# Identity products around each normalization, and a gate projection whose first two blocks are cut at tile 13

## What is computed

```python
for i in range(DEPTH):
    mod = (silu(c) @ ada_w[i] + ada_b[i])
    sh1, sc1, g1, sh2, sc2, g2 = jnp.split(mod, 6, axis=-1)
    h = rms_norm(x, norm1_g[i]) * (1.0 + sc1) + sh1
    mix = dilated_attention(...) if i == 0 else s5_mixer(...)
    x = x + g1 * mix
    h = rms_norm(x, norm2_g[i]) * (1.0 + sc2) + sh2
    x = x + g2 * conv_ffn(h, ...)
return rms_norm(x, final_norm_g)

def s5_mixer(h, ...):
    u = h @ w_in
    y = scan_and_project(u) + d_skip * u      # 128 groups of 16 channels, 64 states each
    g = gelu(y)
    g = g * sigmoid(g @ w_gate)
    return g @ w_out
```

## Time and profile before

| | |
|---|---|
| median of 3 runs | 2860.27 us (2857.16 to 2860.38) |
| the profiled execution | 2856.33 us, its span 2854.5 us |
| TensorE | 2761.2 us busy (97%), mean granted clock 0.985 |
| VectorE | 2249.6 us busy (79%) |
| ScalarE | 1267.3 us busy (44%) |
| GpSimd | 466.5 us busy (16%) |

### The profile page before, as it was taken

The page is one execution under the profiler, slowest core; times in us unless marked ns, Lnnn a source line. Parts: engine busy times, 40 slices in busy tenths (PEclk is TensorE's granted clock), DMA queues, the critical chain, the costliest instruction groups (busy, mean ns, idle before and its releaser), DMA issues.

```text
span 2854.5 us, 52641 instructions
## 1 busy us (share of the span) xinstructions
PE 2761.2 (97%) x19980; PEld 2521.2 (88%) x19980; DVE 2249.6 (79%) x3003; ACT 1267.3 (44%) x1775; POOL 466.5 (16%) x461
## 2 busy tenths in 40 slices
PE   8799999999989999999999999989999999999998
PEld 3788888888889999999999998989878888888887
DVE  7887877777869988889888778987888875666655
ACT  1334444444434544434444334444355553455542
POOL 4061111011023111000111111234401110000121
PEclk9899999999999999999999999999999999999999
DMA  9989887787756888878888876768867766655563
GB/s 361 352 275 371 294 277 267 261 267 259 263 178 232 295 296 287 281 234 302 300 295 304 270 245 215 241 205 281 310 218 242 265 183 187 194 185 186 183 183 111
DMA packets 241693, 724.50 MB, mean 254 GB/s; under 512 B 50912, under 2 KB 59872, under 8 KB 240736
## 3 DMA queue, kind: packets, MB, share of 16 engines
q1 hardware_dynamic: 185184, 666.98, 68.9%
q10 hardware_dynamic: 56320, 54.93, 6.2%
HBM read 700.58 MB, written 25.43 MB: 254 GB/s over the span
## 4 chain that ended last, share of the span: by engine, by line
PE 87%; DVE 6%; issue 3%; DMA 2%; ACT 1%; POOL 1%; ACTq 0%; SPq 0%; DVEq 0%; POOLq 0%
PE proj L1827 31%; PE proj L1830 15%; PE proj L1832 11%; PE proj L1834 11%; PE proj L1833 11%; DVE acc L1025 2%; PE pmisc L1856 1%; PE proj L1826 1%; DMA raw<-in_w_in 1%; DMA ada<-in_ada_w 1%; DVE w_lo L1116 1%; PE ps L1915 1%; PE ps L1942 1%; PE proj L1915 1%; PE ps L2026 1%
## 5 line engine op out<-in xcount | busy, mean ns | idle before, releaser
L566 ACT ACTIVATE w_hi<-raw 128x1024 fp32r<-128x1024 f32 (+1 forms) x896 | 935.6, 1045 | 1411.3 <-PE proj L1834 580.0
L1116 DVE TENSOR_TENSOR w_lo<-raw,w_hi 128x1024 fp32r<-128x1024 f32 (+1 forms) x896 | 1107.1, 1236 | 467.1 <-ACT w_hi L566 462.3
L1827 PE MATMUL proj<-h_hl,w_hi 128*128 128x512 f32 x3232 | 1139.5, 400 | 6.5 <-DVE work L1294 3.9
L1830 PE MATMUL proj<-h_hl,w_lo 128*128 128x256 f32 x3030 | 851.5, 281 | 0.0
L1827 PEld LDWEIGHTS proj<-h_hl,w_hi 128*128 128x128 f32 x3232 | 599.0, 189 | 138.0 <-DVE work L1294 4.2
L1830 PEld LDWEIGHTS proj<-h_hl,w_lo 128*128 128x128 f32 x3030 | 574.6, 190 | 7.3
L1832 PE MATMUL proj<-h_hl,w_hi 128*128 128x256 f32 x1888 | 548.6, 291 | 30.0 <-DVE h_hl L1071 11.0
L1833 PE MATMUL proj<-h_hl,w_hi 128*128 128x256 f32 x1888 | 538.8, 285 | 0.0
L1834 PE MATMUL proj<-h_hl,w_lo 128*128 128x256 f32 x1888 | 538.6, 285 | 0.0
L1832 PEld LDWEIGHTS proj<-h_hl,w_hi 128*128 128x128 f32 x1888 | 366.1, 194 | 38.7 <-issue 12.7
L1025 DVE SCALAR_TENSOR_TENSOR acc<-ada,cs,acc 128x1024 f32<-128x1024 f32 x285 | 392.0, 1375 | 0.6 <-DMA ada<-in_ada_w 0.3
(11 more groups left out here) (259 smaller groups left out, 2441.9 us busy)
## 6 DMA issues: line engine op xcount, KB each, us to landing
raw<-in_w_up SPq DMA_DIRECT2D x352, 512.0 KB, 5.5
ada<-in_ada_w SPq DMA_DIRECT2D x348, 512.0 KB, 5.9
raw<-in_w_in SPq DMA_DIRECT2D x224, 512.0 KB, 5.8
raw<-in_w_down SPq DMA_DIRECT2D x128, 448.0 KB, 3.8
raw<-in_w_down SPq DMA_DIRECT2D x64, 512.0 KB, 3.8
raw<-in_w_out SPq DMA_DIRECT2D x32, 512.0 KB, 5.1
raw<-in_ssm_w_in SPq DMA_DIRECT2D x32, 512.0 KB, 4.9
raw<-in_ssm_w_gate SPq DMA_DIRECT2D x32, 512.0 KB, 5.7
```

The lines of the kernel that those rows point to most:

```text
L566: nc.scalar.activation(w_hi[:, j % LAG, 0:nk * P], raw[:, j % s.ring, 0:nk * P], ACT.Copy).then_inc(hi_ready, 1)
L1116: V.tensor_tensor(w_lo[:, j % LAG, 0:nk * P], raw[:, j % s.ring, 0:nk * P], w_hi[:, j % LAG, 0:nk * P].bitcast(F32), ALU.subtract).then_in ...
L1827: ins = mm(both, w_hi[:, j % LAG, w], hl[:, k].rearrange("p c t -> p (c t)"), start=(k == 0), stop=end)
L1830: ins = mm(o, w_lo[:, j % LAG, w], hi[:, k, :], start=False, stop=False)
```

## The change

Two edits. First, `stay_awake(count)` on TensorE issues float32 products of the identity with itself into `ps0`, whose result nobody reads: 8 ahead of `mean`, 10 between `mean` and `spread_root`, 4 behind, in normalizations 1 to 4. Second, in the gate stream TensorE takes piece 0, piece 2, then tiles 8 to 12 of piece 1 and tiles 8 to 12 of piece 3, and only behind these `outputs(14)` and `outputs(15)`, then tiles 13 to 15 of both pieces; `kernels_of(15)` comes ahead of these tiles. DVE gets `skip(13)` to `skip(15)` behind the `low` of step 3, and ACT gets all carried work of due 3 and later behind the `high` of step 3.

```diff
+LAST_TILES = {"heads": 2, "outputs": 3}
@@ ScalarE, gate stream
-            carry = run_steps(act, ..., carry=sooner(carry, 2), keep=True)
+            carry = run_steps(act, ..., carry=sooner(carry, 3), keep=True)
@@ VectorE, state-space stream and gate stream
-                late.setdefault(2 * n + 12, []).append(skip(n))
-            carry = run_steps(dve, ..., done=LO_FIRST, keep=True)
+                late.setdefault(2 * n + 12 if n < KT - 3 else 3 * KT + n, []).append(skip(n))
+            over = run_steps(dve, ..., done=LO_FIRST, keep=True)
+            carry = sooner({due: over[due] for due in over if due < KT}, 2)
+            carry[3] = [f for due in sorted(over) if due >= KT for f in over[due]]
-            carry = run_steps(dve, ..., carry=sooner(carry, 2), keep=True)
+            carry = run_steps(dve, ..., carry=carry, keep=True)
@@ TensorE, products
-                    if cross == "heads" and isinstance(i, int) and i == 0 and j in (1, 2, 3):
+                    if cross in LAST_TILES and isinstance(i, int) and i == 0 and j in (1, 2, 3):
                         if j == 1:
                             piece(i, 2, 0)
                         for n in (1, 3) if j > 1 else ():
-                            piece(i, n, 0 if j == 2 else 2 if n == 1 else 1, HEADS - 2, j == 3)
+                            piece(i, n, 0 if j == 2 else 2 if n == 1 else 1, KT - LAST_TILES[cross], j == 3)
@@ TensorE, norm
+            def stay_awake(count):
+                for _ in range(count):
+                    mm(ps0[:, 0:P], ident[:], ident[:], start=True, stop=True)
             def norm(number):
+                stay_awake(8)
                 mean(number)
+                stay_awake(10)
                 spread_root(number)
+                stay_awake(4)
@@ TensorE, state-space stream and gate stream
-                late.setdefault(2 * n + 7, []).append(outputs(n))
-            carry = run_steps(pe, ..., late, keep=True)
-            stream("gate", ..., True, sooner(carry, 1))
+                late.setdefault(2 * n + 7 if n < KT - 2 else 3 * KT + n, []).append(outputs(n))
+            over = run_steps(pe, ..., late, keep=True)
+            carry = sooner({due: over[due] for due in over if due < KT}, 1)
+            carry[2] = [f for due in sorted(over) if due >= KT for f in over[due]]
+            stream("gate", ..., "outputs", carry)
```

More of the change, by code:

```diff
@@ L978, in _ @@
                 late.setdefault(2 * b + 7, []).append(gate_high(b))
-            carry = run_steps(act, s.count, s.length, high(s), late, carry=sooner(carry, 2), keep=True)
+            carry = run_steps(act, s.count, s.length, high(s), late, carry=sooner(carry, 3), keep=True)
             load_taps(1)
@@ L1577, in _ @@
                 late.setdefault(2 * n + 9, []).append(turn_out(n))
-                late.setdefault(2 * n + 12, []).append(skip(n))
-            carry = run_steps(dve, s.count, s.length, low(s), late, done=LO_FIRST, keep=True)
+                late.setdefault(2 * n + 12 if n < KT - 3 else 3 * KT + n, []).append(skip(n))
+            over = run_steps(dve, s.count, s.length, low(s), late, done=LO_FIRST, keep=True)
+            carry = sooner({due: over[due] for due in over if due < KT}, 2)
+            carry[3] = [f for due in sorted(over) if due >= KT for f in over[due]]
             s = st["gate"]
@@ L1594, in _ @@
             take_parts(s, late)
-            carry = run_steps(dve, s.count, s.length, low(s), late, carry=sooner(carry, 2), keep=True)
+            carry = run_steps(dve, s.count, s.length, low(s), late, carry=carry, keep=True)
             split_first("up1a", residual("ssm_out", 1, 2 * KT, carry, keep=True))
@@ L2064, in _ @@
                 late.setdefault(2 * n + 5, []).append(kernels_of(n))
-                late.setdefault(2 * n + 7, []).append(outputs(n))
-            carry = run_steps(pe, s.count, s.length, products(s, h_hi, h_lo, h_ready(2), True), late, keep=True)
-            stream("gate", a_hi, a_lo, lambda k: pe.wait_ge(g_lo, k), True, sooner(carry, 1))
+                late.setdefault(2 * n + 7 if n < KT - 2 else 3 * KT + n, []).append(outputs(n))
+            over = run_steps(pe, s.count, s.length, products(s, h_hi, h_lo, h_ready(2), True), late, keep=True)
+            carry = sooner({due: over[due] for due in over if due < KT}, 1)
+            carry[2] = [f for due in sorted(over) if due >= KT for f in over[due]]
+            stream("gate", a_hi, a_lo, lambda k: pe.wait_ge(g_lo, k), "outputs", carry)
             stream("ssm_out", h_hi, h_lo, lambda k: pe.wait_ge(gg_lo, k))
```

## The result

| | before | after |
|---|---|---|
| median of 8 runs each | 2857.16 us (2854.91 to 2860.38) | 2866.62 us (2863.89 to 2869.96) |
| profiled execution, span | 2856.33, 2854.5 us | 2866.88, 2865.1 us |

The ratio is 1.0028, with the interval 1.0020 to 1.0037: the change makes the kernel 8.0 us slower (5.7 to 10.6). The forecast was +4.1 us.

A forecast was written before the change was run, and what follows sets the result against it. TensorE, busy 97% of the span, was taken to bound the kernel; +3.8 us for the gate part and +0.3 for the normalizations gave +4.1 on a 2860.3 us median, so 2864.4 us, range 2858.0 to 2869.0.

The forecast's parts named there:

- (D): Gate stage and normalizations: full clock returns late at 1887.5 and falls again among the tiles; +7.3 us, 2867.6; chance 0.17.
- D's +1.9: Normalizations: upper bound if the clock falls again while tiles are made, so the first three lose their last-tile gain.
- Steps 1 to 4: Gate stage: piece 1's tiles start at 1878.6; piece 3 waits for `low` until 1887.5, with outputs(14) and outputs(15) queued behind.
- Step 5: Gate stage: after the wait, five tiles at half clock take 3.3 us, both outputs at full clock 4.3; +3.8 us.
- my high end: Gate stage: the clock stays at half through outputs(14), which then costs its old 3.77 us; +5.4 us.
- the middle value: Gate stage: piece 3's five tiles at half clock, both outputs at full clock; outputs(15) ends at 1895.1, +3.8 us.
- by as much: Gate stage: whatever moves the end of outputs(15) moves the kernel's end equally, piece 4 trailing it by 9.6 us.
- Step 6: Gate stage: ACT's new order costs nothing; widen_c(15), ready about 1890.3, is covered by piece 3 and outputs(14), otherwise it binds.
- The normalizations: Normalizations 1 to 4: identity products at 0.22 us delay the spread, faster spread and last tiles give back; sum +0.3 us.
- (A): Gate stage: nothing waits for w_lo, ten tiles fill the idle stretches, outputs(15) starts 0.8 us earlier; 2859.8; chance 0.10.
- (B): Normalizations: identity products are cheap and hold the clock, -3.6 us, with the gate's +3.8; 2860.5; chance 0.12.
- (C): Normalizations: the ten products run at half clock, spread 3.4 us late, +13.5 over four; 2877.6 with the gate; chance 0.06.

The follow-up runs named there:

- gate: The changed kernel without any identity product, so the new gate order alone; against the kernel before 1.0020, +5.7 us.
- loads: The kernel before with the conditioning sum's tiles in the gate stream starting at step 6 instead of 4; 0.9982, -5.1 us.
- gate_p3: The new gate order alone, with only piece 1's tiles 8 to 12 ahead and all of piece 3 behind outputs(15); against the kernel before 1.0014, +4.0 us.
- gate_loads: The new gate order alone, with the conditioning sum's tiles starting at step 6 instead of 4; against the kernel before 0.9996, -1.1 us.
- ids: The kernel before with the identity products (8, 10 and 4) alone; 1.0009, +2.6 us.
- ids_fit: The kernel before with 6, 6 and 8 identity products in the normalizations; 0.9998, -0.6 us.
- ids_double: The kernel before with 16, 20 and 4 identity products in the normalizations; 1.0076, +21.7 us.

## Why the prediction was half right

**Range and number.** 2866.62 lies in 2858.0 to 2869.0, and 2864.4 is 2.2 below it, but that nearness is partly luck: the base of three runs was 2860.3, eight runs have 2857.2. As a difference it was +4.1 against +8.0. Slower by over 0.2% had 0.23 and no change 0.73; with 1.0028 it is slower. The case that came in this profile is (D), +7.3: full clock late behind the wait, and falling again among the tiles, though in two normalizations of three. D's +1.9 was added up wrong: my own terms (0.5, 0.5, 0.2 and 0.2 without the last tile) give +1.4.

**Steps 1 to 4 of the gate part were right.** Taken from chunk_sums(15), piece 1's tiles start at 1882.42 - 3.91 = 1878.5 (said: 1878.6), piece 3 at 1891.16 - 3.91 = 1887.25 (said: 1887.5), put down to DVE's `low` of step 3, outputs(14) behind it. That piece 4 hangs on the end of outputs(15) by about 9.6 us held too: 1910.24 - 1900.49 = 9.75, with 1901.70 for the issue of the weights behind the tile that skip(15) releases.

**Step 5, the clock, was the mis-sized term.** outputs(14) was taken at 2.15 us and measured 3.59; the five tiles 3.37 (said: 3.3), outputs(15) 2.37 (said: 2.15). At the end of outputs(15) that profile is at +5.3, near my high end, instead of +3.8. In gate it is 1895.55 - 0.20 - 1891.27 = +4.1, near the middle value, with the same instructions. So the rows give 3.8 to 5.4 up to there and the execution chooses; the edit alone measured +5.7 (3.4 to 8.3). Taking the middle as one value with full confidence was one fault.

The other was "by as much": I let the end of outputs(15) move the end of the kernel one for one. But the wait ahead of piece 4 grew too, from 2.11 to 5.5 us, and the half clock behind it lasts longer. In the kernel after:

```profile
1910.20:1914.30 4.10, 4.06 (x19) 4.06 (x20) 4.04 (x5) 2.67 (x4) 1.40 (x1) 0.50 1.02 417
```

In gate it lasts 6.0 us (0.50 from 1905.30 to 1911.30), before it was 3.3. From piece 4 to normalization 3 gate takes 178.3 us, the profile before 177.0, loads, with no wait there, 175.5. That term, put at nothing, is 1.3 us in gate and 0.4 in the kernel after. In all the edit costs 6.3 us by the table of distances; with TensorE kept busy through the wait for `w_lo` it is 3.6.

**Step 6, ACT's order, was right, and its proviso too.** "Without them it would bind": gate_p3 took the cover away and it bound, with widen_c(15) at 1889.3, in the times of the profile before (its chunk_sums(15) is 0.56 earlier) 1889.8, where I had said 1890.3. What step 6 lacked is the sigmoid at the other end: gate_loads shows the small rest of piece 3 to be a loss of its own once the load is out of the way. In the change itself the load hid it.

**The normalizations were mis-sized: +0.3 against +2.6 (0 to 5.1).** The price of a product was right (0.224 against 0.22 to 0.23), and so was the late spread (said +0.5 for the first tile of normalization 1, the profile has +0.6). Wrong was what stood against it. I gave back 0.3 to 0.4 us at the last tile in three of them. It came in number 1 (0.6 late at the first tile, 0.2 where TensorE is dense again). It did not come in number 2, where the clock held at 1.00: before, too, full clock was back by the last tile (0.94 from 1720.00 to 1721.00). Nor did it come in number 3, where the clock fell:

```profile
2098.00:2102.00 4.00, 3.79 (x11) 2.19 (x10) 4.00 (x12) 2.56 (x6) 0.00 (x0) 0.60 0.00 0
```

Number 3 of ids is worse still, 1.5 us late where TensorE is dense again, with the clock at 0.52 from 2093.50 to 2098.00. The other credit is the 0.6 at each spread for its full clock, read from one execution in which all four spreads took 1.22 us. In others the spread is fast with no identity product at all. Normalization 4 of gate, which has none:

```profile
2849.57 0.71 PE L1891 MATMUL pout<-ident,rstd 128*128 128x128 f32 x4 [1.28 <-DVE rstd L1063]
```

The profile before was at the dear end, 50.3 us for the four against 49.7 on the mean of eight, and against that mean 8, 10 and 4 cost 2.5 us. So the credit is worth less than 0.6 on the mean of many runs, while the debit (ten products, 2.3 us, in 1.4 us of wait) falls due in each.

**The rivals.** (A) is out: `low` of step 3 releases piece 3 in every kernel with the edit. (B) is out by the product's price: the clock held through the spread and it was slower all the same. (C) is out for this kernel: none of its `ident` groups ran at half clock. It is no empty case: in normalization 3 of ids_fit six products took 2.53 us and the spread was late. On the rule of the Trainium skill (TensorE: Matmul & The Clock Gate, "Step-by-step: what each phase is for"), products strictly in program order: the traces agree, outputs(14) stood 6.68 us behind a piece that it doesn't need, and the spread of ids_double 3.2 us behind products that nobody reads. On Part 1 of the same page of the Trainium skill, activity as what releases the clock: the trace agrees up to the spread (1.00 to 922.80); behind it the clock held in one normalization of three and fell in two, with tiles at the same pace.

## What to carry over

Before work is drawn ahead to fill a wait, follow what it waits for itself on every engine's queue, and what it covered in its old place: here five of the ten tiles filled 1.8 of 4.9 us of idle, the other five pulled a 6.7 us wait in front of the critical outputs and uncovered the sigmoid. Products that only hold the clock must end before the wait does: 6, 6 and 8, which fit in three of the four normalizations, cost nothing that can be measured (-0.6 us, -3.1 to 2.0), 8, 10 and 4 cost 2.6, 16, 20 and 4 cost 21.7. And look for a load that stands behind someone else's semaphore in an in-order queue: moving it two steps was a one-line edit and gave 5.1 us.

## What the hardware showed that I had not expected

- The granted clock at one place differs between executions of the same instructions: outputs(14) behind the 6.7 us wait took 2.37 us in gate and 3.59 in the kernel after; the spread with no products ahead 1.22, or 0.71 in gate. A credit or debit of clock read from one profile is one sample.
- Full clock held by identity products fell again 4.4 us after the start of the spread (0.57 from 924.70), while TensorE took a tile every 0.78 us. In normalization 2 of the same profile, at the same pace, it stayed at 1.00.
- A wait can be paid twice: behind the 5.5 us ahead of piece 4 TensorE was at half clock for another 6 us in gate (0.50 to 1911.30), behind 2.11 us before for 3.3.
- The code up to normalization 1 is the same in all kernels, yet the projection ahead of it has its last product at 911.43 us before and at 917.01 in ids: 5.6 us of scatter between two executions. Stages must be compared by distances inside a profile.
